# A macaron decoder step with latent attention: the key weights of the latent space come already turned from the host

## The reference

```python
def mla_project(h, pos, w_dq, q_gain, w_uq, w_dkv, kv_gain, w_uk, qk_gain_q, qk_gain_k):
    cq = rms_norm(h @ w_dq, q_gain)
    q = jnp.einsum('bsr,rhd->bshd', cq, w_uq)                       # 16 heads, 128 + 64 wide
    q = jnp.concatenate([q[..., :NOPE_DIM], rope(q[..., NOPE_DIM:], pos)], axis=-1)
    q = rms_norm(q, qk_gain_q) * qk_gain_k.astype(q.dtype)
    q_lat = jnp.einsum('bshn,chn->bshc', q[..., :NOPE_DIM], w_uk)   # the latent product
    ...
    c = rms_norm(ckv[..., :KV_LORA], kv_gain)
    k_nope = jnp.einsum('bsc,chn->bshn', c, w_uk).astype(jnp.float32)  # the key product
    ssq = jnp.sum(k_nope * k_nope, axis=-1) + ...
    k_scale = lax.rsqrt(ssq / QK_DIM + EPS).astype(h.dtype)
```

## Time and profile before

| | |
|---|---|
| median of 3 runs | 2060.96 us (2057.55 to 2062.87) |
| the profiled execution's own time | 2060.5 us |
| its span in the trace | 2058.9 us |
| PE busy | 2038.1 us (99%) |
| DVE busy | 1608.6 us (78%) |
| ACT busy | 1124.1 us (55%) |
| stage 3, from 1439.4 to 1467.5 us | 28.1 us |

### The profile page before, as it was taken

The page is one execution under the profiler, slowest core; times in us unless marked ns, Lnnn a source line. Parts: engine busy times, 40 slices in busy tenths (PEclk is TensorE's granted clock), DMA queues, the critical chain, the costliest instruction groups (busy, mean ns, idle before and its releaser), DMA issues.

```text
span 2058.9 us, 44454 instructions
## 1 busy us (share of the span) xinstructions
PE 2038.1 (99%) x16716; PEld 1991.5 (97%) x16716; DVE 1608.6 (78%) x2686; ACT 1124.1 (55%) x1948; POOL 364.3 (18%) x437
## 2 busy tenths in 40 slices
PE   9999999999999999999999999999999999999999
PEld 8999999999999999999999999998779999999999
DVE  7779985426467898998899898668776578989998
ACT  6446554433134665655665565446676456656555
POOL 0011111222011111111111111112333221111111
PEclk9999999999999999999999999999999999999999
DMA  5467773231314777876677777543322126777775
GB/s 167 120 159 178 189 195 117 82 102 63 103 63 124 166 178 178 194 184 152 158 182 182 185 183 183 136 133 84 115 73 83 62 62 156 183 178 180 181 179 153
DMA packets 360763, 295.70 MB, mean 144 GB/s; under 512 B 22111, under 2 KB 325260, under 8 KB 360356
## 3 DMA queue, kind: packets, MB, share of 16 engines
q1 hardware_dynamic: 323706, 227.26, 36.7%
q0 software_dynamic: 36592, 66.07, 19.6%
q10 hardware_dynamic: 314, 0.37, 0.1%
HBM read 224.57 MB, written 2.66 MB: 110 GB/s over the span
## 4 chain that ended last, share of the span: by engine, by line
PE 85%; DVE 6%; DMA 5%; issue 2%; ACT 2%; SPq 0%; POOL 0%; DVEq 0%; ACTq 0%; POOLq 0%
PE side L856 28%; PE main L807 26%; PE main L856 20%; DMA raw<-raw 2%; PE side L1390 1%; DMA sums_w<-raw 1%; DVE w_lo L2150 1%; PE main L1139 1%; PE main L1307 1%; PE side L1227 1%; PE side L1349 1%; PE side L1055 1%; PE main L1207 1%; DMA raw<-in_ffn_w_up 1%; DMA raw<-in_ffn_w_gate 1%
## 5 line engine op out<-in xcount | busy, mean ns | idle before, releaser
L856 PE MATMUL side<-xw_hi,w_hi 128*128 128x260 f32 x1344 | 380.8, 283 | 5.0 <-ACT main L1572 2.0
L856 PE MATMUL side<-xw_hi,w_lo 128*128 128x260 f32 x1344 | 381.1, 284 | 0.0
L856 PE MATMUL side<-xw_lo,w_hi 128*128 128x260 f32 x1344 | 380.2, 283 | 0.0
L2150 DVE TENSOR_TENSOR w_lo<-raw,w_hi 128x512 fp32r<-128x512 f32 (+2 forms) x472 | 324.8, 688 | 35.3 <-ACT w_hi L1517 17.4
L856 PE MATMUL main<-xw_hi,w_hi 128*128 128x260 f32 x1008 | 286.1, 284 | 0.0
L856 PE MATMUL main<-xw_lo,w_hi 128*128 128x260 f32 x1008 | 284.7, 282 | 0.0
L856 PE MATMUL main<-xw_hi,w_lo 128*128 128x260 f32 x1008 | 284.5, 282 | 0.0
L856 PEld LDWEIGHTS side<-xw_hi,w_hi 128*128 128x128 f32 x1344 | 253.2, 188 | 7.7 <-ACT main L1572 2.8
L856 PEld LDWEIGHTS side<-xw_hi,w_lo 128*128 128x128 f32 x1344 | 253.2, 188 | 0.0
L856 PEld LDWEIGHTS side<-xw_lo,w_hi 128*128 128x128 f32 x1344 | 252.8, 188 | 0.0
L3091 POOL DMA_DIRECT2D sums_w<-raw x116 | 100.7, 868 | 687.8 <-DMA raw<-in_ffn_w_gate 314.8
(11 more groups left out here) (464 smaller groups left out, 5422.4 us busy)
## 6 DMA issues: line engine op xcount, KB each, us to landing
sums_w<-raw POOLq DMA_DIRECT2D x112, 256.0 KB, 3.3
raw<-raw POOLq DMA_DIRECT2D x112, 256.0 KB, 5.1
raw<-in_ffn_w_gate SPq DMA_DIRECT2D x86, 256.0 KB, 4.6
raw<-in_ffn_w_gate SPq DMA_DIRECT2D x43, 512.0 KB, 5.9
raw<-in_ffn_w_up SPq DMA_DIRECT2D x84, 256.0 KB, 3.9
raw<-in_ffn_w_up SPq DMA_DIRECT2D x42, 512.0 KB, 6.2
raw<-in_gmlp_w_in SPq DMA_DIRECT2D x16, 1024.0 KB, 5.4
raw<-in_ffn_w_down SPq DMA_DIRECT2D x56, 256.0 KB, 4.0
```

Source lines behind the costliest of these rows:

```text
L856: mm = nc.tensor.matmul(into[j], w_tiles(w, weights_at(s, j))[:, k, :], moving[:, k, order[j], :], start=(j in (0, 1) and k == 0 and i == ...
L2150: a = nc.vector.tensor_tensor(dst, src, hi.bitcast(F32), ALU.subtract)
```

## The change

The host lays `w_uk` out a second time as n x head x c (`laid_out`), as a new input of 1 MB. SP loads it into `wuk_t`, which now holds all 16 heads, between the loads of `trig` and of the page list. ACT multiplies it by `gg` in place in four operations of 128x512, which stand behind the tiles u = 3, 9, 15 and 16 of the query projection. The 16 turns on PE, the 16 copies on ACT and their waits (`wuk_turned`, `wuk_copied`) are gone. PE waits once for all four operations (`wuk_scaled`), ahead of the first key product.

```diff
-def program(nc, x_prompt, x_sample, cache_mla, ...
+def program(nc, w_uk_turned, x_prompt, x_sample, cache_mla, ...
...
-        wuk_t = sb("wuk_t", [P, 2, P], F32, proj)
+        wuk_t = sb("wuk_t", [P, H, P], F32, proj)
...
             sp.dma_start(trig[:].rearrange("p a n -> p (a n)"), table[:, N_CONST:N_CONST + N_TRIG]).then_inc(kv_in, 16)
+            sp.dma_start(wuk_t[:], w_uk_turned).then_inc(wuk_in, 16)
             sp.dma_start(pages[:], page_table.rearrange("b n -> (b n)").unsqueeze(0)).then_inc(pages_in, 16)
...
-            def turn_wuk(h):
-                if h >= 2:
-                    pe.wait_ge(wuk_copied, h - 1)
-                nc.tensor.transpose(side[:, 2 + h % 2, 0:P], wkv[:, h, :], ident).then_inc(wuk_turned, 1)
-
-            turn_wuk(0)
             pe.wait_ge(row_copied, QB + 1)
             pe.wait_ge(kv_lo_set, 4)
+            pe.wait_ge(wuk_scaled, 4)
             for h in range(H):
-                if h + 1 < H:
-                    turn_wuk(h + 1)
...
-                pe.wait_ge(wuk_copied, h + 1)
                 for half in range(2):
-                    mm = nc.tensor.matmul(main[:, h % 2, half, 0:HALF], wuk_t[:, h % 2, :],
+                    mm = nc.tensor.matmul(main[:, h % 2, half, 0:HALF], wuk_t[:, h, :],
...
-                if y == 1:
-                    pe.wait_ge(wuk_copied, H)
...
+                elif part == 3 and c < 3 or u == 16:
+                    if u == 3:
+                        act.wait_ge(wuk_in, 16)
+                    q0 = 12 if u == 16 else 4 * c
+                    quarter = wuk_t[:, q0:q0 + 4, :]
+                    nc.scalar.activation(quarter, quarter, ACT.Copy, scale=gg[:, 0:1]).then_inc(wuk_scaled, 1)
...
-                act.wait_ge(wuk_turned, h + 1)
-                if h >= 2:
-                    act.wait_ge(lat_done, h - 1)
-                nc.scalar.activation(wuk_t[:, h % 2, :], side[:, 2 + h % 2, 0:P], ACT.Copy,
-                                     scale=gg[:, 0:1]).then_inc(wuk_copied, 1)
...
+def laid_out(inputs):
+
+    return dict(w_uk_turned=inputs["mla_w_uk"][0].transpose(2, 1, 0))
```

More of the change, by code:

```diff
@@ L125, in halves, with program @@
     return ap.rearrange("p (h n) -> p h n", h=2)
-def program(nc, x_prompt, x_sample, cache_mla, page_table, norm_g, ffn_w_gate, ffn_w_up, ffn_w_down,
+def program(nc, w_uk_turned, x_prompt, x_sample, cache_mla, page_table, norm_g, ffn_w_gate, ffn_w_up, ffn_w_down,
             gmlp_w_in, gmlp_b_in, gmlp_v_norm, gmlp_w_s, gmlp_b_s, gmlp_w_out,
@@ L403, in program @@
         q_ssq_read = sem("q_ssq_read")
-        wuk_turned = sem("wuk_turned")
-        wuk_copied = sem("wuk_copied")
+        wuk_in = sem("wuk_in")
+        wuk_scaled = sem("wuk_scaled")
         kn_done = sem("kn_done")
@@ L3273 @@
     arrays, args = {}, []
-    for name in INPUTS:
-        a = np.ascontiguousarray(inputs[name])
+    for name, a in {**laid_out(inputs), **{name: inputs[name] for name in INPUTS}}.items():
+        a = np.ascontiguousarray(a)
         arrays[f"in_{name}"] = a
```

## The result

The changed kernel takes 2065.27 us (median of 20 runs, 2059.88 to 2070.39) against 2060.57 us (20 runs, 2057.55 to 2065.05): a ratio of 1.0017, 95% interval 1.0010 to 1.0025. That is under the 0.3% that count as a difference, but it is no gain, and it lies above the predicted range. The profiled execution took 2068.42 us and had a span of 2066.8 us, 7.9 us longer than before's.

A forecast was written before the change was run, and what follows sets the result against it. PE was taken to bound the kernel, busy for 99% of the span. Turns -0.6, tail -0.05, scaling 0 and transfer 0 summed to -0.65 us: 2060.3 us from the median, range 2057.5 to 2063.5 us.

The forecast's parts named there:

- What bounds the kernel: PE, busy for 99% of the span; only time taken off its sequence or added to its waits counts.
- the turns: Stage 3, 16 turns off PE: heads 0 to 2 give nothing, heads 3 to 8 give 0.6 us.
- the tail: Stage 3, heads 9 to 15: DVE's copy decides, 1.97 to about 1.96 us a pair, giving some 0.05 us.
- The excess of head 8: Stage 3: head 8's extra 0.24 us, PE waiting for ACT's copy, goes, but head 9 waits for DVE anyway.
- The rival with 1.78 us: Stage 3: the tail is not bound by DVE, all 1.78 us come back, 2059.2 us; chance 0.13.
- The scaling: Four operations on ACT in the query projection, at most 2.9 us in all, hidden in idle time: 0 us.
- The transfer: SP's extra load delays the first `w_uq` chunk by about 5 us, hidden; everything later on SP keeps its time.
- The cover: Ahead of ACT's split of the first `w_uq` chunk: 6.9 us between the chunk's landing and its use.
- The sum: Whole kernel: 0 - 0.6 - 0.05 + 0 + 0 = -0.65 us, giving 2060.3 us from the median.
- something that I have not seen: Anywhere in the kernel: chance 0.06 for an effect outside the named cases, no size given.

The follow-up runs named there:

- before_busy3: Kernel before, its twelve narrow starting matmuls on TensorE written as three wide ones, making the stream 36 instructions shorter: 2062.26 us against 2060.67 (ratio 1.0003).
- after_pad48: Changed kernel plus 24 tiny unread turns on TensorE ahead of stage 3's first head, stream 1 instruction shorter than before's: 2061.18 us against 2061.41 (ratio 0.9998).
- after_busy3: Changed kernel, its twelve starting matmuls written as three wide ones, stream 85 instructions shorter than before's: 2058.54 us (ratio 0.9986), repeated 2058.01 us (0.9980).
- before_start36: Kernel before with three wide starting matmuls plus nine tiny ones, which restore its stream's length: 2060.47 us against 2061.12 (ratio 1.0001).
- after_start36: Changed kernel with three wide starting matmuls plus nine tiny ones, stream 49 instructions shorter than before's: 2061.99 us against 2061.12 (ratio 1.0000).

## Why the prediction was wrong

- **What bounds the kernel, the turns, the tail.** Right. The step of a head was 2.27 us (2.28 predicted), the pairs of the tail came 1.94 us apart (1.96), and the weight loads there waited for DVE's copy. The Trainium skill's rule on early weight loads (page "TensorE: Matmul & The Clock Gate", section "Step-by-step: what each phase is for") was estimated to give 0.33 us more in the tail. The trace again shows the load waiting. Stage 3 gave 0.86 us where the sum had 0.65 (0.81 to 0.88 in the seven other traces whose heads have no turns). The missing 0.2 us are small excesses: the step fell by 0.12 us six times instead of 0.10, since a pair of key products takes 1.38 us instead of 1.40, and the tail gave 0.10 instead of 0.05. The excess of head 8 is lost to DVE, as predicted: from the last pair of key products to head 9's weight load it is 1464.57 - 1461.18 = 3.39 us, before 1460.40 - (1456.87 + 0.11) = 3.42. The rival with 1.78 us is refuted.
- **The scaling.** Right: 0.71 us each (at most 0.73 had been taken), no new wait of PE in the query projection.
- **The transfer.** Right that it is hidden: measured from PE's pair, the chunk behind it is there 4.1 us later, where about 5 had been taken. Two readings were off. The cover was 6.4 us and not 6.9, since 3.7 us is the median of eight loads and the load in question took 4.2. And not everything later on SP kept its time: the cached pages are issued 1.1 us later (the first at 1370.78, before at 1364.76, in a trace that is 4.90 late there), which cost nothing.
- **The step that failed** is "The sum": it holds everything outside stages 1 to 3 for unchanged, with 0.06 for "something that I have not seen". The turns were priced by PE's time alone. They were also 49 instructions, with their waits, and by leaving they moved a fetch of TensorE's instructions, some 580 us later, from 0.40 to 3.11 us behind the first load of a weight tile. That cost 2.1 to 2.9 us of waiting in most traces and 1.7 us of lower clock. That the place of the fetch makes this stall is shown in the traces: without the change (`before_busy3`), taken back (`after_pad48`) and passed by (`after_busy3`). In the times only the changed program with the new start resolves it.
- **The size.** The first measurement said 4.7 us, the repeat 2.9 us with an interval that takes in no loss, and the same stream with its input last 0.7 and 0.4 us, not resolved either. In the traces, matched matmul by matmul, the stretch from 2030 us to the end is longer than before's by 4.0 us on the mean in the seven with a late third load and by 0.6 us in the eleven with the fetch outside. The difference of 3.4 us less stage 3's 0.86 leaves an estimate of 2.5 us. The rest of the first number is not settled, nor is whether other fetches, which moved as well, cost anything in other stretches. Why a packet of about 1 us delays a load by some 2 us the records don't show either.

## What to carry to other kernels

Here 33 to 85 instructions fewer on TensorE moved a later instruction fetch by 3 to 7 us, and with 33 to 49 fewer it landed in a load that had just had time enough: after such an edit, look at the whole span, not at the touched stage. To tell such a shift from the edit itself, give the instructions back as idle ones, or take as many out of the old kernel elsewhere; here that told more than the times, which wander by 2 to 3 us. And a gain that was eaten can be had back: the change and the start in 36 instructions fewer are together 2.1 to 3.1 us faster than before, of which the start alone (`before_start36`) gave 0.65 us, not resolved.

## What the hardware showed unexpectedly

- Instruction fetches stand among the weights' packets in the DMA view: packets of 16 KB that took 0.92 to 1.75 us in the tile looked at, and with them in a load the fourth load landed 5.0 to 5.9 us behind its issue instead of 3.6 to 4.4.
- The fetch isn't free at before's place either. In the eight traces in which it starts between 0.25 us ahead of SP's first load and 0.52 us behind it, SP's issue of the second load takes 0.68 to 1.47 us, and 0.49 to 0.50 us in the twelve others. Before:

```profile
2027.61 1.32 SPq L606 DMA_DIRECT2D sums_w<-in_ffn_w_down  x1
```

- The start can have a fall of the clock as well: 0.67 granted on average from 10 to 15 us before, and none in `before_busy3`, whose wide matmuls stand in place of the narrow ones. Of the fifteen traces with the narrow ones ten have that fall, of the five with the wide ones none, so the narrow ones favour it and don't force it. It is a part of what the times wander by: at 20 us the ten traces without it are 0.3 to 1.5 us ahead of before.

```profile
10.00:15.00 5.00, 5.00 (x29) 4.67 (x30) 3.39 (x7) 2.90 (x5) 0.00 (x0) 0.67 1.10 351
```

```profile
10.00:15.00 5.00, 4.54 (x37) 4.32 (x37) 4.22 (x9) 3.19 (x5) 0.00 (x0) 1.00 1.10 351
```

- The clock fell to 1.2 GHz between 1440 and 1443 us, for 3.4 us (once 6.8), in four of the five traces with tiny turns ahead of stage 3, and in none of the other fifteen but `after_start36`, which has no such turns there. So the turns favour it and aren't needed for it; what decides stays open.
